# Two output tiles instead of one inside the norms of a two-layer diffusion block

## The reference

```python
def rms_norm(x, g):
    xf = x.astype(jnp.float32)
    y = xf * lax.rsqrt(jnp.mean(xf * xf, axis=-1, keepdims=True) + RMS_EPS)
    return (y * g.astype(jnp.float32)).astype(x.dtype)

# per layer, for the context stream and the latent stream alike
hx = modulate(rms_norm(x, p["g_norm1"]), mod_x[0], mod_x[1])      # h * (1 + scale) + shift
zr_x, zm_x, zf_x, zg_x = jnp.split(hx @ p["w_in"], IN_SPLITS, axis=-1)
...
hx2 = modulate(rms_norm(x_mid, p["g_norm2"]), mod_x[3], mod_x[4])
x_new = x_mid + mod_x[5] * swiglu(hx2, p["w_ffn_in"], p["w_ffn_out"])
```

## Time and profile before

| | us |
|---|---|
| median of three runs | 2486.52 |
| the three runs | 2484.43, 2492.95, 2486.52 |
| the profiled execution | 2487.39 |
| its span (first to last instruction) | 2485.6 |
| TensorE matmuls busy | 2196.0 (88%) |
| DVE busy | 1312.9 (53%) |
| ACT busy | 927.3 (37%) |
| mean granted TensorE clock | 0.938 of full |

### The profile page before, as it was taken

One profiled execution on the slowest core, in us unless ns is written; L12 is line 12 of the kernel. 1 busy time (PEld: TensorE's weight loads), 2 busy tenths in 40 slices (PEclk: granted clock), 3 DMA queues, 4 the chain that ended last, 5 costly groups with the idle time before them and its releaser, 6 DMA issues. The chain is left out here.

```text
span 2485.6 us, 47863 instructions
## 1 busy us (share of the span) xinstructions
PE 2196.0 (88%) x19929; PEld 1732.0 (70%) x19929; DVE 1312.9 (53%) x1958; ACT 927.3 (37%) x1605; POOL 346.0 (14%) x445
## 2 busy tenths in 40 slices
PE   6897688879989998889998987968888798998998
PEld 2374688845557887668887833837888566997998
DVE  5756777772372333343332267477777515455544
ACT  4633344422342222232222156334444234444442
POOL 1001533300100011010000011024333020010000
PEclk9999899987999999999999988989999879998999
DMA  8640000030111332222232375400000302453543
GB/s 283 237 144 1 2 0 2 0 113 20 34 37 51 96 100 85 68 85 88 100 102 85 102 235 185 144 1 1 0 2 1 131 1 87 137 177 122 184 164 125
DMA packets 157295, 219.47 MB, mean 88 GB/s; under 512 B 6815, under 2 KB 123769, under 8 KB 156129
## 3 DMA queue, kind: packets, MB, share of 16 engines
q1 hardware_dynamic: 155648, 215.74, 25.7%
q0 software_dynamic: 1504, 1.71, 0.2%
HBM read 208.00 MB, written 9.44 MB: 87 GB/s over the span
## 5 line engine op out<-in xcount | busy, mean ns | idle before, releaser
L332 DVE TENSOR_TENSOR W_low<-RING,W_high 128x1024 fp32r<-128x1024 f32 x364 | 445.0, 1231 | 483.1 <-ACT W_high L329 482.5
L329 ACT ACTIVATE W_high<-RING 128x1024 fp32r<-128x1024 f32 x364 | 380.4, 1053 | 663.0 <-PE BANK L370 628.5
L368 PE MATMUL BANK<-H_high,W_high 128*128 128x512 f32 (+2 forms) x1472 | 526.1, 357 | 77.7 <-ACT H_high L584 35.7
L370 PE MATMUL BANK<-H_high,W_low 128*128 128x512 f32 (+2 forms) x1472 | 519.6, 353 | 0.0
L369 PE MATMUL BANK<-H_low,W_high 128*128 128x512 f32 (+2 forms) x1472 | 519.6, 353 | 0.0
L368 PEld LDWEIGHTS BANK<-H_high,W_high 128*128 128x128 f32 (+1 forms) x1472 | 283.2, 192 | 132.5 <-issue 51.7
L370 PEld LDWEIGHTS BANK<-H_high,W_low 128*128 128x128 f32 (+1 forms) x1472 | 283.5, 193 | 37.9
L369 PEld LDWEIGHTS BANK<-H_low,W_high 128*128 128x128 f32 (+1 forms) x1472 | 284.0, 193 | 36.9 <-issue 1.1
L1169 PE MATMUL BANK<-RING,WORK 64*64 64x64 f32 x4096 | 165.9, 220 | 17.3 <-DVE RING L1122 8.7
L1169 PEld LDWEIGHTS BANK<-RING,WORK 64*64 64x64 f32 x4096 | 144.8, 135 | 29.8 <-issue 29.6
L974 POOL TENSOR_TENSOR WORK<-WORK,masks 128x256 f32<-128x256 f32 x160 | 126.7, 804 | 113.2 <-PE BANK L1169 112.7
(11 more groups left out here) (277 smaller groups left out, 3412.2 us busy)
## 6 DMA issues: line engine op xcount, KB each, us to landing
RING<-w_mod_dram SPq DMA_DIRECT2D x48, 1024.0 KB, 5.0
RING<-w_in_dram SPq DMA_DIRECT2D x46, 1024.0 KB, 5.1
RING<-w_ffn_in_dram SPq DMA_DIRECT2D x44, 1024.0 KB, 5.0
RING<-w_ffn_out_dram SPq DMA_DIRECT2D x22, 1024.0 KB, 4.7
RING<-w_out_dram SPq DMA_DIRECT2D x8, 1024.0 KB, 5.0
h_high<-H_high SPq DMA_DIRECT2D x2, 2048.0 KB, 6.4
h_low<-H_low SPq DMA_DIRECT2D x2, 2048.0 KB, 11.9
H_high<-h_high SPq DMA_DIRECT2D x2, 2048.0 KB, 10.7
```

The lines of the kernel that those rows point to most:

```text
L329: high_ready.mark(nc.scalar.activation(self.part(0, c), self.raw(c), ACT.Copy))
L332: low_ready.mark(nc.vector.tensor_tensor(self.part(1, c), self.raw(c), self.part(0, c).bitcast(FP32), ALU.subtract))
L368: nc.tensor.matmul(out, w[0], x[0], start=start, stop=False)
L370: return nc.tensor.matmul(out, w[1], x[0], start=False, stop=stop)
```

## The change

In `norm` TensorE applies each channel tile of the normalised stream to two output tiles of the next projection, each in its own bank, so 6 matmuls for each k where there were 3. The banks are 0 and 1 where `project_rwkv` follows, and 0 and 2 where `ffn_in` follows (its gate tile uses bank 0, its up tile bank 2). The wait for weights asks for two chunks. The stage behind raises two signals by `count` and starts at output tile 2.

```diff
-    def norm(scale, shift, t0, ahead, save=False):
+    AHEAD_TILES = 2
+
+    def norm(scale, shift, t0, ahead, banks, save=False):
...
-                w0 = ahead.part(0, 0), ahead.part(1, 0)
-                pe.wait_ge(*low_ready(1))
+                weights = [(ahead.part(0, c), ahead.part(1, c)) for c in range(AHEAD_TILES)]
+                pe.wait_ge(*low_ready(AHEAD_TILES))
                 for k in range(DT):
...
-                    product3(BANK[:, 0, 0:n], [x[:, k] for x in w0], [x[:, k, t0:] for x in HS], k == 0, k == DT - 1)
+                    for w, bank in zip(weights, banks):
+                        product3(BANK[:, bank, 0:n], [x[:, k] for x in w], [x[:, k, t0:] for x in HS], k == 0, k == DT - 1)
...
-                product.count(pe)
-                for m in range(1, Z_TILES):
+                for m in range(AHEAD_TILES):
+                    product.count(pe)
+                for m in range(AHEAD_TILES, Z_TILES):
...
-                pe_sig.count(pe)
+                for c in range(AHEAD_TILES):
+                    (product if c % 2 else pe_sig).count(pe)
                 for u in range(FT):
                     for g in range(2):
-                        if u + g == 0:
+                        if 2 * u + g < AHEAD_TILES:
                             continue
...
-        norm(scale_1, mod[:, 0], 0, w_rwkv, save=True)
+        norm(scale_1, mod[:, 0], 0, w_rwkv, (0, 1), save=True)
...
-        norm(scale_2, mod[:, 3], t0, w_ffn_in)
+        norm(scale_2, mod[:, 3], t0, w_ffn_in, (0, 2))
```

## The result

| | before | after |
|---|---|---|
| median of six runs, us | 2488.36 | 2474.57 |
| lowest to highest, us | 2482.57 to 2498.26 | 2469.82 to 2479.20 |
| the profiled execution, us | 2487.39 | 2479.20 |
| its span, us | 2485.6 | 2477.4 |
| matmuls busy in the span, us | 2196.0 | 2199.9 |

The medians differ by 13.8 us. The ratio of the runs is put at 0.9941, with a 95% interval of 0.9917 to 0.9965: 14.7 us faster (9 to 21).

What follows compares the result with a forecast made beforehand. TensorE was taken to bound the stages behind norms, and slower producers the norms. Savings of 13.55 us in three norms plus 2.0 in the last, less 0.4 for counts, gave 15.1 us: 2471.4 us, range 2467 to 2478.

Steps and rivals of the forecast that it cites:

- the late clock: Rival, 15%: in every norm the clock rises only 8.05 us after the first matmul; 9.3 us saved, 2477.2.
- (a): Stages behind the norms: each loses 24 matmuls, 3 x 5.45 + 2.88 = 19.2 us removed.
- (b): Three 512-token norms: 24 added matmuls lengthen them by 0.8, 1.0 and 1.0 us; 13.55 us saved net.
- this sign of the forecast: Expected in the profile of a norm's product: the clock rises 4.6 to 5.0 us after the first matmul.
- The r of a norm: Time from a norm's first matmul to the clock's rise, taken as before: 4.6 or 5.0 us; last norm 4.9.
- (c): Last norm: product ends 8.0 us after its start, growth 1.2 us; 2.0 us saved with its following stage.
- (d): Waits: the second weight chunk's costs nothing; the second `count` at each change of stage costs 0.1 us, 0.4 in all.
- (e): Stages behind: chunk 3 due earlier but hidden, thinnest margin 0.5 us in last `ffn_in`; busier TensorE does not slow producers.
- the last norm gave its 2 us: Rival, 10%, said the last norm gives nothing: its weights, low clock and thin margin use up 2.0 us; 2473.4.
- the tile was on the path: Rival, 5%, said the tile removed from the stages behind was not on the path; 2487 to 2491.
- The clock stayed up: Rival, 3%, said the clock stays low in the norms, with matmuls alternating between two banks; 2496.
- One argument: Against a low clock in the norms: it stayed at 1.00 after its rise with TensorE busy 4.67 of 7.80 us.

Runs made afterwards that it cites:

- e3: Changed kernel with the second tile's 24 matmuls placed behind all of the first's in each norm; ratio to the kernel before 1.0006.
- f1: The changed kernel measured and profiled once more, with nothing altered; ratio to the kernel before 0.9946.
- f2: Changed kernel (two tiles) plus 30 unused matmuls per norm ahead of the first channel tile to hold the clock up; ratio to the kernel before 0.9951.
- e2: Changed kernel with two tiles only in the norms ahead of `ffn_in`, one ahead of `project_rwkv`; ratio to the kernel before 0.9970.
- e4: Changed kernel with three tiles instead of two in each norm; ratio to the kernel before 1.0006.
- f4: Changed kernel with the two banks alternating at every matmul instead of every three; ratio to the kernel before 0.9937.
- e1: Changed kernel with two tiles only in the norms ahead of `project_rwkv`, one ahead of `ffn_in`; ratio to the kernel before 0.9970.
- f3: Kernel before (one tile) plus 30 unused matmuls per norm ahead of the first channel tile to hold the clock up; ratio 1.0018.

## Why the prediction was right

The forecast was 15.1 us of gain and 2471.4; measured were 2474.57, 3.2 above it and inside the range. The stretches show 15.3 us of gain, the medians 13.8, the ratios of the two measurements 14.7 and 13.4. The 2471.4 stood against the median of three runs, and the median of six of the kernel before lies 1.8 higher. The runs alone, with an interval of 9 to 21, could not tell the forecast from the late clock's 9.3 us; the stretches do. That their sum comes within 0.2 us of the forecast is partly luck, as some of the terms show.

- (a) What leaves: right. e3, which moves the 24 matmuls and hides none, is 0.9 us from before, so a matmul removed behind and added in a norm balance to the pitch.
- (b) Growth of the 512-token norms: forecast 0.8, 1.0 and 1.0, without the count. Measured, with 0.15 for the count taken off: 0.83, 1.00 and 0.72. The third is the producers' bound; its clock rose 3.6 us after the start and not 5.0, so this sign of the forecast (4.6 to 5.0) did not hold there. The r of a norm is not its own: in f1 the three came at 5.1, 4.3 and 3.5. Taking each as it had been was luck within 0.3 us; that it matters so little is what f2 shows. How 5.45 us of work fits where the idle times of the first norm's product add up to only 3.3 us is seen from the pitch. About 9 matmuls at 0.427, 15 at 0.2275 and the 0.13 at the start are 7.4 us of work in a product of 12.3: by this estimate 4.9 us are free, and 4.7 were filled (4.55 and the count). The view shows less, since a matmul's duration runs beyond its pitch.
- (c) The last norm: r taken as 4.9, measured 4.7; growth forecast 1.2, measured 1.08 (8.63 less 7.40 less 0.15). The 4.9 was taken from norms whose own r then varied by 1.6 us, so that it came so near is luck too. Saved 1.95 with the count, against 1.9.
- (d) Counts: 0.15 each, 0.6 in all, against 0.4 taken and a bound of 0.45 each. The weights' wait cost nothing.
- (e) Half right. Chunk 3: in the last `ffn_in` its low part started at 2277.89 and was ready at 2279.12, 2.2 us into the stage, needed at 2.9. TensorE did not wait. But the thinnest margin is not there: it is at chunk 5, which (e) took to follow its lists, and which hangs on the transfer of its weights. In the changed kernel 0.46 us were left, and in e2 0.4 us were lost. Timeline of DVE, chunk 3:

```profile
2277.89 1.23 DVE L332 TENSOR_TENSOR W_low<-RING,W_high 128x1024 fp32r<-128x1024 f32 x1 [4.86 <-ACT W_high L329]
```

  In e4, where the cover is gone, the wait was 3.9 us in `project_rwkv` and 2.8 in either `ffn_in`, and the clock fell with it. That a busier TensorE does not slow the producers held: the cell product takes 536 ns in the mean before and 537 after. (Its mean and its longest of 966 belong beside the 474 and 471 that the forecast read.) ACT's longest wait for a tile in `project_rwkv` is 4.8 us, as before.
- The rivals: the late clock did not come in any of the two-tile profiles; the last norm gave its 2 us, 1.5 in e2; the tile was on the path (e3). The clock stayed up despite the alternating banks (f4 sharpens this), so the Trainium skill's warning (TensorE: Matmul & The Clock Gate, "A second HAM failure mode: psum-queue depth-cycling") does not apply to switching banks as such. What it says of short idle times between groups does fit e1 and f3, but there it is the kernel with one tile and one bank that starves (waits of up to 1.2 us in f3).
- One argument was weaker than it read: that the clock had stayed at 1.00 with TensorE busy 4.67 of 7.80 us was true of that profile, not of the code. In e1, e2, e3 and f3 the same one-tile product lost the clock. So the kernel before may have in some executions a loss that the change takes away, 2.8 us in e1. It lost the clock in four of nine products and lost time by it in one; how much of the measured gain that is stays open, and the profile of the kernel before has none of it.

## What to carry to other kernels

Where an engine starves at a steady rate behind slower producers, give it a second consumer of what has arrived, and first work out the ceiling: the length of the starved stretch less its matmuls at their pitch, and not the sum of the idle times shown. Two tiles filled it here; a third brought no gain and exposed a wait that two had covered. Look then at every input of the next stage that comes due earlier, not only at the first: here the first (chunk 3) kept 0.7 us, but the third (chunk 5) 0.46 and in e2 nothing. The work has to go between the waits; in the same stage but behind them it is worth nothing. Compare stretches that hold only what was changed when untouched stages scatter by as much as the effect.

## What the runs showed of the hardware

- Starving by short waits is enough to take TensorE's clock from 2.4 to 1.2 GHz. In the norms of f3 no wait inside the product was longer than 1.2 us, the engine was busy 53 to 56% of the time, and the clock fell in three of three; in e1 it was busy 1.95 of 3.50 us ahead of the fall. With a second tile in the waits (f2) it stayed at 1.00 in three of three. It does not happen each time: in the kernel before the clock stayed up with TensorE busy 4.67 of 7.80 us.
- A single wait of 3.9 us between dense work made the clock fall for 6.8 us, and 2.5 us were lost behind it (e4). In the same run the clock also fell shortly after two waits of 2.8 us, for about 3.4 us. A wait on TensorE can cost more than its length.
- One and the same kernel had profiled spans 14 us apart, with granted clocks of 0.937 and 0.944, the difference lying between the stretches, 12.0 us of it in the first layer's scan and its preparation, at a mean granted clock of 0.91 and 0.94. What decides it was not tried.
